# A decoder step on one core: K units among other tiles, self heads between the scan's steps, value tiles and output tiles behind them

## The reference, cut to what matters

```python
# attention over a paged cache (8 heads of 64) for the sample, causal "self" heads for the prompt
# scan, per chunk of 128 prompt tokens (the sample is one chunk of 4 tokens per sequence):
acum = jnp.cumsum(dtc * a, axis=2)
seg = acum[:, :, :, None, :] - acum[:, :, None, :, :]
lmat = jnp.where(causal, jnp.exp(jnp.where(causal, seg, 0.0)), 0.0)
scores = jnp.einsum('bcihn,bcjhn->bcijh', cc, bc) * lmat
y_diag = jnp.einsum('bcijh,bcjh,bcjhp->bcihp', scores, dtc, xc)
chunk_states = jnp.einsum('bcjhn,bcjh,bcjhp->bchpn', bc, decay_end * dtc, xc)
# s_final by a scan over chunks from s0 (state_ssm for the sample, zero for the prompt)
y_off = jnp.einsum('bcihn,bchpn,bcih->bcihp', cc, s_in, jnp.exp(acum))
y = rmsnorm((y_diag + y_off + xs * d_skip) * silu(z), norm_w)
h = h + concat[y, attention] @ w_out
```

## Time and profile before

| | us |
|---|---|
| three runs | 791.22, 789.61, 785.44 |
| median | 789.61 |
| profiled execution | 791.33, span 789.5 |
| TensorE busy, of the span | 709.1 |
| stretches: K units / V units and heads / end and barrier / scan | 118.7 / 124.9 / 10.6 / 105.5 |

### The profile page before, as it was taken

The page is one execution under the profiler, slowest core; times in us unless marked ns, Lnnn a source line. Parts: engine busy times, 40 slices in busy tenths (PEclk is TensorE's granted clock), DMA queues, the critical chain, the costliest instruction groups (busy, mean ns, idle before and its releaser), DMA issues. The chain is left out here.

```text
span 789.5 us, 12071 instructions
## 1 busy us (share of the span) xinstructions
PE 709.1 (90%) x4351; PEld 543.4 (69%) x4351; DVE 415.8 (53%) x905; ACT 142.0 (18%) x322; POOL 120.5 (15%) x200
## 2 busy tenths in 40 slices
PE   4879999997999997889879997868999999999993
PEld 2456677785756674543326775537999999999992
DVE  2253244243876821884387222536788887445524
ACT  2131114222101021431111000411211111000002
POOL 3120001003002002200034110003254444000000
PEclk9969999999899999796979998989999999999998
DMA  9563677687779955400006790456354444544401
GB/s 285 135 178 100 207 241 254 224 264 210 220 232 288 294 142 138 137 1 1 1 0 165 235 320 0 147 174 213 108 159 145 145 150 152 186 161 161 160 1 61
DMA packets 102492, 126.18 MB, mean 160 GB/s; under 512 B 6385, under 2 KB 78565, under 8 KB 102440
## 3 DMA queue, kind: packets, MB, share of 16 engines
q1 hardware_dynamic: 99240, 115.08, 46.5%
q0 software_dynamic: 3200, 10.39, 4.6%
HBM read 117.14 MB, written 8.31 MB: 159 GB/s over the span
## 5 line engine op out<-in xcount | busy, mean ns | idle before, releaser
L843 PE MATMUL ps<-hw,wring 128*128 128x288 f32 x576 | 152.3, 426 | 5.7 <-DVE qs L1692 3.7
L843 PEld LDWEIGHTS ps<-hw,wring 128*128 128x128 f32 x576 | 114.5, 200 | 42.4 <-DVE qs L1692 4.1
L1646 DVE COPY tmp<-ps 128x512 f32<-128x512 f32 (+3 forms) x84 | 53.6, 643 | 67.3 <-PE ps L829 61.4
L829 PEld LDWEIGHTS ps<-ident,big 128*128 128x128 f32 x400 | 45.6, 146 | 37.2 <-issue 13.1
L829 PE MATMUL ps<-ident,big 128*128 128x128 f32 x400 | 58.6, 289 | 10.0 <-DVE tmp L1646 6.3
L1441 ACT ACTIVATE tmp<-ps 128x512 f32<-128x512 f32 (+4 forms) x71 | 39.7, 562 | 131.4 <-PE ps L829 111.3
L1239 PE MATMUL ps<-hw,wring 128*128 128x144 f32 x256 | 35.5, 294 | 2.2 <-DVE hw L1649 2.2
L709 POOL TENSOR_TENSOR acc<-acc,sq 128x288 f32<-128x288 f32 (+1 forms) x35 | 27.9, 798 | 52.9 <-ACT sq L1447 50.8
L1239 PEld LDWEIGHTS ps<-hw,wring 128*128 128x128 f32 x256 | 33.7, 196 | 2.7 <-DVE hw L1649 2.7
L1239 PE MATMUL ps<-big,wring 128*128 128x144 f32 x256 | 34.0, 286 | 0.0
L866 PE MATMUL ps<-big,wring 128*128 128x288 f32 x128 | 32.6, 408 | 0.5 <-DVE big L1649 0.5
(11 more groups left out here) (306 smaller groups left out, 1177.1 us busy)
## 6 DMA issues: line engine op xcount, KB each, us to landing
wring<-in_w_in SPq DMA_DIRECT2D x16, 1024.0 KB, 6.9
big<-in_cache_k SPq DMA_DIRECT2D x64, 256.0 KB, 2.7
big<-in_cache_v SPq DMA_DIRECT2D x64, 256.0 KB, 3.5
wring<-in_w_up SPq DMA_DIRECT2D x16, 1024.0 KB, 5.3
wring<-in_w_down SPq DMA_DIRECT2D x16, 1024.0 KB, 5.0
wring<-in_w_out SPq DMA_DIRECT2D x8, 768.0 KB, 8.7
wring<-in_w_ca_kv SPq DMA_DIRECT2D x4, 1024.0 KB, 5.3
big<-in_state_ssm SPq DMA_DIRECT2D x8, 512.0 KB, 6.1
```

The lines of the kernel that those rows point to most:

```text
L829: last = pe.transpose(ps[0:c, bank(key), col:col + r], in_, ident[0:r, 0:r])
L843: last = pe.matmul(ps[:, t % 2, 0:width], w, rhs(c * k_tiles + k), start=(c + k == 0), stop=(c == chunks - 1 and k == k_tiles - 1))
L1646: dve.tensor_copy(dst, src).then_inc(turn_dve, 1)
```

## The change

SEQ is rewritten; the entries are now single tiles and steps.
- The memory transposes (`memt`) come first, then tab, qk0, m0, and the first root. K units stand among qk, m and x pairs (K11, K12 and K13 behind x0, x1 and x2). The v pairs go to the end of the input projection.
- The sample chunk of the scan is cut up and laid between z and v tiles, ahead of the prompt chunks (CHUNKS is 2, 0, 1). Its state transposes and reads are done in batches of four turns, the reads of a batch one behind another at four different column positions.
- The eight self heads, with their scores in turn banks, and V units 00 to 03 stand between the steps of prompt chunks 0 and 1. The gate reads the output sums where they lie in PSUM.
- `out` is split: `oz`, the scan's part (w_out rows 0 to 1023), with V units 10 to 13 between its pairs, and then `oa`, the attention part. `oz` tiles are scaled by the root and added to h, `oa` tiles afterwards. The first barrier is gone.
- A turn's evictor is now given by key: decay, sums and exponentials to ScalarE; gram, outputs, self scores and updates to VectorE; only the rest alternate.
- SP loads a weight block when the one four blocks back is used up, and pages two units ahead. POOL stores each half of the states once its updates are done, ahead of the bias rows of the first heads.

The diff, cut to its core. The order of the heads and scan steps, the reads and updates, the stores and the outputs:

```diff
+    tile("v", 0, 1)
+    item("upd", 7, 11)
+    item("tok", 0)
+    item("upd", 11, 14)
+    tile("v", 1, 0)
+    item("upd", 14, 16)
+    item("sums", 0)
+    tile("v", 1, 1)
+
+    item("bias")
+    item("seg", 0, 0)
+    item("kvtok", 0, 2)
+    item("seg", 0, 1)
     item("heads_in", "self")
-    pair("x", 0, 1)
...
+    item("yo", 0, 0)
+    item("seg", 0, 2)
+    item("yo", 0, 1)
+    item("head", "self", 0)
+    item("seg", 0, 3)
+    item("yo", 0, 2)
+    item("head", "self", 1)
+    item("yo", 0, 3)
+    item("sst", 0)
+    item("kvtok", 2, 3)
+    item("head", "self", 2)
+    item("tok", 1)
+    item("sums", 1)
+    item("seg", 1, 0)
+    item("head", "self", 3)
+    item("seg", 1, 1)
     unit("V", 0, 0)
-    item("head", "self", 0)
-    pair("x", 1, 1)
+    item("yo", 1, 0)
+    item("head", "self", 4)
+    item("seg", 1, 2)
+    item("yo", 1, 1)
+    item("head", "self", 5)
     unit("V", 0, 1)
-    item("head", "self", 1)
-    pair("x", 2, 1)
+    item("seg", 1, 3)
+    item("yo", 1, 2)
+    item("zsq", 0)
+    item("head", "self", 6)
+    item("yo", 1, 3)
+    item("sst", 1)
+    item("zsq", 1)
+    item("zsq", 2)
+    item("zsq", 3)
+    item("head", "self", 7)
     unit("V", 0, 2)
...
+            def load_block(g):
+                key = BLOCKS[g]
                 if g >= SLOTS:
-                    old = BLOCKS[g - SLOTS]
-                    if old in USED:
-                        sp.wait_ge(chunk_used, USED[old] + 1)
-                    else:
...
-                    for c in range(s[3]):
-                        if BLOCK[s[1:3] + (c,)] >= done:
-                            load_block(s[1:3] + (c,))
-                elif s[0] == "unit":
-                    load_unit(s[1:])
-                elif s[0] == "ssd":
-                    load_unit(("ST", 0))
-                    load_unit(("ST", 1))
+                if s[0] == "tile" and s[3] == 1:
+                    g = BLOCK[s[1:3]]
+                    if g + SLOTS < N_BLOCKS:
+                        load_block(g + SLOTS)
+                elif s == ("sums", 0):
+                    load_unit(UNIT[("V", 0, 0)])
...
+            def store_states(h):
+                src = kvring[:, UNIT[("ST", h)] % 2].rearrange("p b a (c n) -> p b (a c) n", n=SN)
+                turned(pool, ("up", 8 * h + 7))
+                for b in range(GB):
+                    store(O["sample_ssm"][h * GB + b].rearrange("(c p) n -> p c n", p=P), src[:, b], st_out[h])
+
             for s in SEQ:
-                if s[0] == "early":
-                    add_squares(1, NP_)
-                elif s == ("heads_in", "self"):
-                    in_ps(pool, ("mvtok", 1))
+                if s[0] == "memt":
+                    add_squares("mem", NP_)
+                elif s[0] == "bias":
+                    turned(pool, ("up", 15))
                     pool.wait_ge(rb_out, 16)
                     load_bias(0), load_bias(1)
                 elif s[0:2] == ("head", "self") and s[2] + 2 < H:
...
+            def outputs(q, hg):
+                slot = seg_no(q, hg) % 2
+                pe.wait_ge(mix_made, seg_no(q, hg) + 1)
+                if q == 1:
+                    pe.wait_ge(cs_made, hg + 1)
+                    if hg == 0:
...
+                    last = pe.matmul(out, xtok[:, h * 64:h * 64 + 64], E4[:, slot, j * P:(j + 1) * P],
+                                     start=True, stop=(q == 0), tile_position=(0, 64 * (j % 2)))
+                    if q == 1:
+                        last = pe.matmul(out, st0[:, h * 64:h * 64 + 64], CS[:, hg % 2, j * P:(j + 1) * P],
+                                         start=False, stop=True, tile_position=(0, 64 * (j % 2)))
+                last.then_inc(turn_ps, 1)
+
...
+            def state_turn(k):
+                bi, bh, g = k // 4, k // 2 % 2, k % 2
+                st = kvring[:, UNIT[("ST", bh)] % 2, bi].rearrange("p a (c n) -> p (a c) n", n=SN)
+                transposes(("state", k), [(st[:, 4 * g + j, :], j * P) for j in range(4)])
+
+            def state_read(k):
+                bi, bh, g = k // 4, k // 2 % 2, k % 2
+                r = 32 * (2 * bh + g)
+                pe.matmul(ps[r:r + 32, 7, :], cz[:, g, GB * bh + bi, :], ssT[k % 8], start=(bi == 0), stop=(bi == 3),
+                          tile_position=(0, r)).then_inc(ssT_used, 1)
+
+            def update(k):
+                bh, c = divmod(k, 8)
+                key = ("up", k)
+                bank_free(pe, key)
+                pe.matmul(ps[:, bank(key), :], xwt[0:NS, c * P:(c + 1) * P], bbd[0:NS, c // 4, GB * bh:GB * bh + GB, :],
+                          start=True, stop=True).then_inc(turn_ps, 1)
...
+
+                    for k in range(0, 20, 4):
+                        if k < 16:
+                            for i in range(k, k + 4):
+                                state_turn(i)
+                        if k == 4:
+                            pe.wait_ge(cz_made, 1)
+                        if k >= 4:
+                            for i in range(k - 4, k):
+                                turned(pe, ("state", i))
+                            for i in range(k - 4, k):
+                                state_read(i)
...
+                if EVICTOR[key] != "dve":
                     return
                 in_ps(dve, key)
-                target_free(dve, key)
...
                                       rs[:, NP_:T].rearrange("p (b i) -> p b i", b=NB), ALU.mult).then_inc(dense_out, 1)
+                elif kind == "oz":
+                    step(dve.tensor_tensor(zpart, ps[:, b, 0:T], rs[:, :], ALU.mult))
+                    dve.tensor_tensor(h3[:, c, :], h3[:, c, :], zpart, ALU.add).then_inc(dense_out, 1)
+                    dve.wait_ge(dense_out, t + 1)
...
+            def gate(q, hg):
+
+                off, n = TOKS[q]
+                key = ("y", q, hg)
+                in_ps(dve, key)
+                if q == 0 and hg == 0:
+                    dve.wait_ge(z_silu, 1)
+                for j in range(2):
+                    c = 2 * hg + j
+                    last = dve.scalar_tensor_tensor(ybuf[:, hg % 2, j * P:(j + 1) * P], xc[:, c, off:off + n],
+                                                    dec[:, c, NB:NB + 1], ps[:, bank(key), j * P:(j + 1) * P],
+                                                    ALU.mult, ALU.add)
+                last.then_inc(turn_dve, 1)
+                turned(dve, key)
+                zz = z[:, 2 * hg:2 * hg + 2, off:off + n]
+                dve.tensor_tensor(zz, zz, heads(ybuf[:, hg % 2, :], 2, P), ALU.mult).then_inc(y_used, 1)
+
```

More of the change, by code:

```diff
@@ L110, in make_plan, with pair, tile @@
     seq = []
-    def pair(kind, n, chunks):
-        seq.append(("pair", kind, n, chunks))
+    def pair(kind, n):
+        seq.append(("tile", kind, n, 0))
+        seq.append(("tile", kind, n, 1))
+    def tile(kind, n, half):
+        seq.append(("tile", kind, n, half))
     def unit(*a):
@@ L154, in make_plan @@
-    pair("x", 2, 1)
+    pair("x", 3)
+    item("probs", 0)
+    pair("x", 4)
+    unit("ST", 0)
+    unit("ST", 1)
+    pair("x", 5)
+    item("dt")
+    tile("z", 0, 0)
+    item("dt_series")
+    tile("z", 0, 1)
+    item("dt_rates")
+    tile("z", 1, 0)
+    item("silu_x")
+    tile("z", 1, 1)
+    tile("z", 2, 0)
+    item("cv")
+    item("tok", 2)
+    tile("z", 2, 1)
+    item("sums", 2)
+    tile("z", 3, 0)
+    item("seg", 2, 0)
+    item("stt")
+    tile("z", 3, 1)
+    item("silu_z")
@@ L187, in make_plan @@
+    pair("caq", 0)
+    item("ss", "ca")
+    pair("caq", 1)
     item("meet")
@@ L231, with seg_no, last_out @@
+_last = {}
+for t in TILE:
+    BANK[t] = (4, 5)[t[2]] if t[0:2] == ("m", 0) else sum(1 for k in BANK.values() if k < 2) % 2
+    IN_BANK[t] = _last.get(BANK[t])
+    _last[BANK[t]] = t
 N_HEADS = {"self": H, "cross": CROSS}
 HEAD0 = {"self": 0, "cross": H}
-def turn(key):
+CHUNKS = [2, 0, 1]
+PLACE = {q: p for p, q in enumerate(CHUNKS)}
+def seg_no(q, hg):
+    return 0 if q == 2 else 1 + 4 * q + hg
+def last_out(q, hg):
+    k = seg_no(q, hg) - 2
+    return ("yd", 1) if k <= 0 else ("y",) + divmod(k - 1, 4)
@@ L259, in plan_turns @@
         elif s[0] == "own":
-            turn(("own", s[1]))
+            turn(s)
         elif s[0] == "probs":
@@ L288, in plan_turns @@
             turn(("pt", s[1], s[2]))
+            if s[1] == "self" and s[2] + 2 < H:
+                turn(("hs", s[2] + 2), "dve")
         elif s[0] == "heads_end":
@@ L351, in build @@
         attT = sb("attT", [P, 4, T])
+        vT = attT
         mkv = sb("mkv", [P, 2048])
@@ L1529, in _ @@
+            for c in range(DT):
+                leave(("x", c))
+                if c:
+                    turned(act, ("x", c - 1))
+                    square("x", c - 1, h3[:, c - 1, :], T)
+            leave("vec")
+            turned(act, ("x", DT - 1))
+            square("x", DT - 1, h3[:, DT - 1, :], T)
             for s in SEQ:
```

1406 lines of the change are left out of this document (692 added, 714 removed).

## The result

Four runs of the changed kernel took 798.74 to 801.89 us, median 800.3, beside 790.41 for the kernel before in the same place: a ratio of 1.014, 95% interval [1.0109, 1.0172]. A second set of six runs gave 1.0151 [1.0121, 1.0181]. So it is slower by 1.4 to 1.5% (9.9 us between the medians of the first set, 12.7 in the second). The range on record, 771 to 807, holds it; its likeliest value, 792, is 8 too low, and "within 1%" was given 0.45 where "slower by over 1%" came.

What follows compares the result with a forecast made beforehand. TensorE was taken as the bound up to 303.4 us, engine chains in the scan; stretches ending at 76.7, 219, 313.5 and 405.0, plus 65.1, put the query tile at 470.1, +2.7 on 789.6: 792 us, range 771 to 807.

Steps and rivals of the forecast that it cites:

- the query tile: First tile of the cross attention's queries, nothing changed behind it: forecast to start at 470.1 us against 467.45, +2.7.
- Start, +2.8: Up to unit K00: qk0 starts 10.0 us later, so K00 starts at 76.7 where the same work ended at 73.9.
- Convolution in front of K turns, +6.6: K11 to K13 beside x tiles: the fourth turn waits 2.2 us for VectorE's copy behind a convolution, three times.
- Reads, -10: Sample part's state reads: sixteen in groups of four cost 3.7 us instead of 13.7.
- Updates, "TensorE pays its matmuls only": Sample part's state updates, laid beside z and v tiles, cost TensorE only their matmuls, 13.7 us.
- The forecast 94.5: From x5's end to the last value tile's end: z tiles, sample part and value tiles, 86.3 us plus 8.2 idle.
- Scan steps and heads, 91.5: Last value tile to first output tile: a chain between engines, 9.5 + 49.5 + 4 + 6.5 + 22 us.
- The upper end for the loads, 14: VectorE's first self head starts 14 us behind the last value tile if its bias load stands behind all stores; 9.5 expected.
- Output tiles, 65.1: First output tile to first query tile: 65.1 us, including a low clock of 2.5 twice.
- Rival two: TensorE falls to the 1.2 GHz level among scan steps and heads: +14, stretch 106, 806 us (800 to 815); chance 0.22.
- Rival one: VectorE's heads overlap TensorE's decays: scan and heads take 75, total 771 us (767 to 781); chance 0.28.
- Rival three: Banks come free in time beside x tiles, so K turns do not wait: 785 us; chance 0.08.

Runs made afterwards that it cites:

- K turns' run: The changed kernel with ScalarE evicting the first three and the sixth of eight turns in K11, K12 and K13, VectorE the others; 795.1 us, ratio 1.009.
- single reads: The changed kernel with one state read behind every group of four transposes, as before, in place of four reads in a row; 816.7 us, ratio 1.0357.
- 128 rows: The changed kernel with its state update matmuls over 128 rows, 96 of them zero, in place of 32; 796.9 us, ratio 1.0114.
- 32 rows there: The kernel before the change with its update matmuls over 32 rows instead of 128; 796.98 us beside 789.87, ratio 1.0085.
- the root early: The changed kernel with the root of the scan's norm ahead of the final state's transposes and V03; 801.7 us, ratio 1.0121.
- no waits: The changed kernel without the loads of bias_rows, VectorE adding memory keys in their place; 794.3 us, ratio 1.007.
- root in the middle: The changed kernel with K turns' evictors, early bias rows, exponentials' order, 128-row updates, and the root between final state's transposes and last head's values; 775.7 us, ratio 0.9838.
- exponentials' order: The changed kernel with ScalarE's exponentials of heads 2, 5, 6 and 7 behind the following scan step's exponential; 801.1 us, ratio 1.0148.

## Why the prediction was right or wrong

**What bounds the kernel; the query tile as the yardstick.** Right as to the sum: of the 10.5 us by which the span grew, 11.1 came ahead of this tile and -0.6 behind it. "Nothing behind it is changed" holds for the work and not for the time: the cross attention was 3.1 shorter and the rest 2.5 longer.

**Start, +2.8.** Too much: it cost 0.1. qk0 came 8.0 later, at 34.3, and not 10.0.

**Convolution in front of K turns, +6.6.** The wait came as forecast (2.2 forecast, 2.23 measured, three times); the slow clock behind two of them, some 3 us (K11 and K12 at 0.84 in the mean, K13 at 1.00), stood only at the upper end. The K turns' run shows that it is the evictor's doing: 8.6 of the 10 us that the three units cost went with it.

**Reads, -10.** Right: 11.7 between the run with single reads and the changed kernel, for transposes and reads together; the sum had 11.4 for both, and 11.9 came.

**Updates, "TensorE pays its matmuls only".** This is the step that failed. 13.7 is sixteen matmuls of 512 columns at the full clock, 0.86 each as a read, and the tiles between them were priced at 3.93, the full clock too. The diff has the rows' change in plain sight (`xwt[0:NS, ...]`), and I took it for a memset saved. In the changed kernel's trace the sixteen updates take 18.6 in all, and three value tiles behind them 6.3 more than the price. The forecast 94.5 was 86.3 of work and 8.2 of idle time; it came as 99.1 and 2.0. With 128 rows and the clock at 1.00 the same stretch is 88.9 and 3.4, 92.2 in all: the work was priced nearly right for that clock, and the idle time too high, which hid part of the error. The runs with 128 rows here and with 32 rows there show it from both sides: 8.9 and 7 us.

**Scan steps and heads, 91.5.** Right in its chain: 10.9, 60.1 and 25.0 for 9.5, 60.0 and 22. What the tail lacked is the order of TensorE's list: the final state's transposes wait 5.72, and the root's matmul stands behind them, the last values and V03 at 407.40, though POOL's sums are there by some 398 (the run with the root early). The upper end for the loads, 14, with the bias rows behind every store, was an estimate of mine that no run tests by itself; it was not reached, the first head started 10.9 behind the last value tile.

**Output tiles, 65.1.** 62.1: the low clock behind the first wait did not come, and the first pair took 8.08, at 0.98; the second came, smaller than forecast (17.35 for 15.7, at 0.91, 1.6 and not 2.5).

**Rival two**, TensorE at a clock near 0.50 in the heads' stretch, had the sign but not the place. Its stretch took 96.0 and not 106, at 0.84 in the mean, and the low clock cost more, 8.9 against 3.6 behind the bias waits, in the stretch that I had priced at the full clock. It took a gap at every step as the cause. Behind the bias waits this trace agrees (no waits, 1.00; waits, 0.82). For the updates it does not: 128 rows for 32 bring the clock of the z/v stretch from 0.89 to 1.00 with no bank changed and with more idle time, 3.4 for 2.0. **Rival one** fell: with the losses mended (root in the middle) the stretch is 84.6 from the start of the last value tile, 80.6 from its end, and not 75. **Rival three** fell with the three waits of 2.23.

**The chances.** 0.25 for slower was too little. The stretches came 3.1, 6.5 and 4.5 longer than forecast, and the start and the output tiles 2.7 and 3.0 shorter: that the sum is only 8 off is in part luck. Most errors of the clock go one way: idle time and the updates over 32 rows were followed by slow work (0.62 behind the K turns' first wait, 0.50 behind the bias waits, 0.61 and 0.50 behind the updates), and I had priced this only in the output tiles, where it was too much.

Open is why the cross attention takes 60.6 or 64.8 us with the same instructions, and why few rows go with a low clock: the runs show that they do, not by what.

## What to carry to other kernels

Cut the profile at the points where the new order changes, and price work at the clock that its own neighbours will leave it, not at the one of the rows it comes from (tiles of one form took 4.15 ahead of the updates and 5.65 to 6.79 behind them). Here some waits on TensorE cost more than their length (9.1 of bias waits, 12.7 of stretch; K11 and K12, 2.23 of wait, 3.9 each), others their length alone (K13, 2.23 of wait, 2.2). Before taking zeros out of a matmul's operand, look at the granted clock around it: in both kernels here 32 rows for 128, in the same 512 columns, cost more (8.9 and 7 us).

## What the runs showed of the hardware

- Update matmuls over 32 rows ran at 0.50 from 396 to 420 us with TensorE busy 23.56 of 24.0; over 128 rows (96 of them zero) at 0.79 with 20.11 busy; in the changed kernel the window with 128 rows, 273 to 309, had 1.00, those with 32 rows 0.61 (276 to 280) and 0.50 (288 to 292, 304 to 308).
- Four reads at four column positions, each 32 columns wide, end in 1.07 us; one by one (single reads) a read takes 1.04 to its end, and a step with four transposes 1.56, of which their 0.66 leave 0.9.
- In the changed kernel and its variants the cross attention, the same in all of them, takes 60.6 to 60.7 us in five profiled executions, 64.7 to 64.9 in five others and 61.7 in one, at a mean clock of 0.97, 0.89 and 0.94: two windows of the changed kernel in the first of the two fences, and the same places of the kernel with the exponentials' order in the second:

```profile
508.55:514.55 6.00, 5.79 (x56) 4.03 (x55) 3.49 (x8) 1.20 (x2) 0.00 (x0) 1.00 0.41 127
532.55:538.55 6.00, 3.20 (x24) 1.36 (x16) 1.40 (x4) 0.86 (x2) 0.39 (x2) 1.00 0.01 3
```

```profile
504.35:510.35 6.00, 5.79 (x49) 3.38 (x48) 1.38 (x2) 1.79 (x3) 0.00 (x0) 0.72 0.04 2
528.35:534.35 6.00, 6.00 (x32) 3.35 (x33) 1.12 (x2) 0.98 (x2) 0.79 (x4) 0.72 0.01 3
```
